# A two-layer decoder trunk: the first two gate/up units of stages 2 to 4 computed in token rows from split weights

## What is computed

```python
x = post_norm(x, 0.5 * swiglu(x, gate[0,0], up[0,0], down[0,0]), ...)   # stage 1
x = post_norm(x, pool_mixer(x), ...)
x = post_norm(x, 0.5 * swiglu(x, gate[0,1], up[0,1], down[0,1]), ...)   # stage 2
x = post_norm(x, 0.5 * swiglu(x, gate[1,0], up[1,0], down[1,0]), ...)   # stage 3
x = post_norm(x, swa_sink_attention(x), ...)
x = post_norm(x, 0.5 * swiglu(x, gate[1,1], up[1,1], down[1,1]), ...)   # stage 4
# swiglu(x) = (silu(x @ gate) * (x @ up)) @ down; gate, up 1024 x 2816, down 2816 x 1024
# post_norm(x, s) = layer_norm(sqrt(2) * x + s), per token over the 1024 channels
```

## Time and profile before

| | |
|---|---|
| median of three runs | 879.35 us |
| profiled execution, its own time | 879.61 us |
| its span, first to last instruction | 877.8 us |
| PE busy | 850.1 us (97%) |
| DVE busy | 561.1 us (64%) |
| ACT busy | 415.5 us (47%) |
| mean granted clock of TensorE | 0.995 |

### The profile page before, as it was taken

How to read it: one execution, slowest core, us unless ns; L and a number is a source line. 1 busy time by engine, 2 the same in 40 slices (tenths; PEclk the granted TensorE clock), 3 DMA queues, 4 the chain that set the end, 5 groups by cost and what they waited for, 6 DMA issues and landing times.

```text
span 877.8 us, 12580 instructions
## 1 busy us (share of the span) xinstructions
PE 850.1 (97%) x4712; PEld 727.4 (83%) x4712; DVE 561.1 (64%) x782; ACT 415.5 (47%) x654; POOL 25.6 (3%) x51
## 2 busy tenths in 40 slices
PE   7999999996999999999999999999989999999996
PEld 6888888886988888888888888887756988888885
DVE  2765565579655655657665655669787856656556
ACT  2555455432354554543454554554564544545540
POOL 0000000001100000001000000011000000000000
PEclk9999999999999999999999999999999999999998
DMA  9986547282585465563756556554145385565501
GB/s 280 351 295 224 184 155 230 72 266 97 193 295 181 160 226 177 168 223 109 238 197 203 180 191 194 189 192 144 49 139 197 104 301 174 189 200 182 191 1 49
DMA packets 116143, 162.19 MB, mean 185 GB/s; under 512 B 3936, under 2 KB 97632, under 8 KB 116112
## 3 DMA queue, kind: packets, MB, share of 16 engines
q1 hardware_dynamic: 112656, 152.06, 52.1%
q0 software_dynamic: 2496, 9.44, 3.1%
q10 hardware_dynamic: 960, 0.27, 0.1%
HBM read 160.70 MB, written 1.05 MB: 184 GB/s over the span
## 4 chain that ended last, share of the span: by engine, by line
PE 91%; DVE 6%; issue 1%; ACT 1%; DMA 1%; DVEq 0%; SPq 0%
PE ps L1083 28%; PE ps L1081 16%; PE ps L1034 10%; PE ps L1036 10%; PE ps L1035 10%; PE ps L1050 6%; PE ps L1080 4%; PE ps L1062 1%; PE ps L907 1%; PE ps L910 1%; PE ps L1115 1%; PE ps L916 1%; DVE xn L740 1%; DVE stats L746 1%; DMA raw_g<-in_ffn_w_gate 1%
## 5 line engine op out<-in xcount | busy, mean ns | idle before, releaser
L1083 PE MATMUL ps<-xT,g_hi 128*128 128x512 f32 x1064 | 379.3, 396 | 0.0
L1081 PE MATMUL ps<-xT,g_lo 128*128 128x256 f32 x1216 | 314.1, 279 | 0.0
L1081 PEld LDWEIGHTS ps<-xT,g_lo 128*128 128x128 f32 x1216 | 229.2, 188 | 12.8
L1083 PEld LDWEIGHTS ps<-xT,g_hi 128*128 128x128 f32 x1064 | 199.7, 188 | 41.2
L690 DVE TENSOR_TENSOR g_lo<-raw_g,g_hi 128x1024 fp32r<-128x1024 f32 x171 | 208.0, 1222 | 25.0 <-ACT g_hi L434 24.9
L700 DVE TENSOR_TENSOR gu<-ps,gu 128x512 f32<-128x512 f32 x76 | 52.6, 692 | 230.5 <-ACT gu L457 230.5
L434 ACT ACTIVATE g_hi<-raw_g 128x1024 fp32r<-128x1024 f32 x172 | 179.7, 1052 | 8.0 <-PE ps L916 3.7
L457 ACT ACTIVATE gu<-ps 128x512 f32<-128x512 f32 x76 | 45.6, 600 | 283.2 <-PE ps L1083 283.2
L1034 PE MATMUL ps<-d_hi,hT_hi 128*128 128x512 f32 x352 | 137.9, 392 | 0.6 <-DVE hT_lo L710 0.6
L1036 PE MATMUL ps<-d_hi,hT_lo 128*128 128x512 f32 x352 | 137.0, 389 | 0.0
L1035 PE MATMUL ps<-d_lo,hT_hi 128*128 128x512 f32 x352 | 137.0, 389 | 0.0
(11 more groups left out here) (128 smaller groups left out, 628.8 us busy)
## 6 DMA issues: line engine op xcount, KB each, us to landing
raw_d<-in_ffn_w_down SPq DMA_DIRECT2D x87, 512.0 KB, 4.0
raw_g<-in_ffn_w_gate SPq DMA_DIRECT2D x43, 1024.0 KB, 5.5
raw_g<-in_ffn_w_up SPq DMA_DIRECT2D x43, 1024.0 KB, 8.0
raw_g<-in_attn_w_qkv SPq DMA_DIRECT2D x6, 1024.0 KB, 6.2
raw_d<-in_attn_w_o SPq DMA_DIRECT2D x8, 512.0 KB, 3.7
gb<-in_ln_g POOLq DMA_DIRECT2D x6, 512.0 KB, 3.8
gb<-in_ln_b POOLq DMA_DIRECT2D x6, 512.0 KB, 5.5
xn<-in_x SPq DMA_DIRECT2D x2, 512.0 KB, 5.9
```

The lines of the kernel that those rows point to most:

```text
L1081: last = pe.matmul(bank[:, S:2 * S], w_lo, xT_hi[:, k, :], start=False, stop=False)
L1083: last = pe.matmul(bank, w_hi, xT[:, k, :, :], start=False, stop=k == KT - 1)
```

## The change

Units 0 and 1 of stages 2 to 4 no longer use raw weights. Their weights are split like the others, into two slots, one of them a new third slot of `g_hi` and `g_lo`; `gate_up_tokens` computes both units together for 128 tokens at a time, tokens on the partitions, 512 moving columns (2 units, gate and up, 128 channels each). ACT and DVE form h in token rows, PE transposes h (two transposes per t) into ACC[0][0], and ACT and DVE split it from there. PE then runs half of gate_up(2) before and half after the second pair of transposes. The copies into `xf` go in stages 2 to 4. Buffers are shared anew to make room (xf lies in qT, kd, rtmp, prevT and pT0 in kx, pT1 in gb, q_sb is halved), so the output bias is loaded into gb during attention, its `residual_bias` moves behind the chunks of q, and the layer-norm offset is loaded when the last values are done. `load_gate_up` of a stage is issued ahead of its first `load_down`.

Where the two new splits stand in the queues of ACT and DVE: for stage 2 after the pool mixer's `residual_bias` and ahead of its layer norm; for stage 3 and for q, k, v in unit 20 of the stage before, the second behind the `d_split` of unit 21 and ahead of unit 21's silu and h; for stage 4 in attention tasks 6 and 7. POOL's half split for q, k, v goes to ACT and DVE too.

```diff
-G_SLOTS = 2
+EXTRA = 2
+G_SLOTS = 3
+        def next_splits(f, u, it):
+            if 1 <= u < UNITS - 2:
+                return [(f, u + 2, it)]
+            if f in (1, 2) and u == UNITS - 2:
+                return [(f + 1 if f == 1 else None, v, 0) for v in range(2)]
+            return []
 # ACT, g_split: when the slot is free
-                    after(act, g_used, (G0[f] + u - 3 if f is not None and u < 4 else G - 1) + 4 * it)
+                    if f is None:
+                        after(act, g_used, G_QKV + (-1, 0, 0, 1, 3, 4)[u])
+                    elif f == 0:
+                        after(act, g_used, 0 if u < 4 else G - 1 + 4 * it)
+                    else:
+                        after(act, g_used, G0[f] + (-1, 0, 0, 2)[u] if u < 4 else G - 1 + 4 * it)
 # ACT and DVE, unit(): one split as before, the second at its end
                 if u + 1 < UNITS:
                     d_split(D0[f] + u + 1, it)
+                for a in ahead[1:2]:
+                    g_split(*a)
 # ACT, attention
+                if i >= len(TASKS) - 2:
+                    if i == len(TASKS) - 2:
+                        act.activation(sm[:, 0, 5, 0:1], mhalf[:, :], ACT.Silu)
+                    g_split(3, i - len(TASKS) + 2)
 # DVE, attention
-            chunk(1, 0)
-            chunk(1, 1)
+            dve.wait_ge(b_o_in, 16)
+            for t in range(TT):
+                chunk(1, t)
+                residual_bias(t, gb[:, 0, :])
...
+                if i >= len(TASKS) - 2:
+                    g_split(3, i - len(TASKS) + 2)
 # DVE, after the pool mixer
-                    layer_norm(1)
-                    for t in range(TT):
-                        x_lo(1, t)
-                    g_split(1, RAW_UNITS)
+                    g_split(1, 0)
+                    g_split(1, 1)
+                    enter(1)
+            def enter(f):
+                e = FFN_EVENT[f]
+                layer_norm(e, between=lambda: x_lo(e, 0))
+                x_lo(e, 1)
+                h_tokens(f, 0)
+                g_split(f, RAW_UNITS)
 # PE
+            def gate_up_tokens(f, t):
+                e, first = FFN_EVENT[f], g_slot(f, 0)
+                out_, tok = ps[:, WORK + 2 + t, :], slice(t * P, (t + 1) * P)
+                w_hi, w_lo = (b[:, first:EXTRA + 1:EXTRA - first, :].rearrange("p u (m k f) -> p u m k f", m=2, k=KT) for b in (g_hi, g_lo))
+                if t == 0:
+                    pe.wait_ge(g_lo_done, 2 * (X0[f] + 2))
+                for k in range(KT):
...
+                    pe.matmul(out_, xT_hi[:, k, tok], w_hi[:, :, :, k, :], start=k == 0, stop=False)
+                    pe.matmul(out_, xT_hi[:, k, tok], w_lo[:, :, :, k, :], start=False, stop=False)
+                for k in range(KT):
...
+                    last = pe.matmul(out_, xT_lo[:, k, tok], w_hi[:, :, :, k, :], start=False, stop=k == KT - 1)
-                    gate_up_raw(f, 0, 0)
-                    gate_up_raw(f, 1, 0, (0,))
+                    gate_up_tokens(f, 0)
                     transposes(e, 1)
-                    gate_up_raw(f, 1, 0, (1,))
-                    gate_up_raw(f, 0, 1)
-                    gate_up_raw(f, 1, 1)
-                ffn_down(f, 0)
+                    gate_up_tokens(f, 1)
+                    h_transposes(f, 0)
+                    gate_up(f, 2, ms=(0,))
+                    h_transposes(f, 1)
+                    gate_up(f, 2, ms=(1,))
+                    ffn_down(f, 0)
 # POOL
+                    gp.wait_ge(oT_ps, len(TASKS))
+                    load_offset(4)
```

More of the change, by code:

```diff
@@ L463, in unit @@
             def unit(f, u, it=0):
-                ahead = (f, u + 2, it) if 1 <= u < UNITS - 2 else (None, 0) if f == 2 and u == UNITS - 2 else None
+                ahead = next_splits(f, u, it)
                 if u not in DIRECT:
                     low_of(f, u, it)
-                if ahead and u not in DIRECT:
-                    g_split(*ahead, halves=(0,))
+                    for a in ahead[0:1]:
+                        g_split(*a, halves=(0,))
                     silu_of(f, u, it)
-                    g_split(*ahead, halves=(1,))
+                    for a in ahead[0:1]:
+                        g_split(*a, halves=(1,))
                 else:
                     silu_of(f, u, it)
-                    if ahead:
-                        g_split(*ahead)
+                    for a in ahead[0:1]:
+                        g_split(*a)
                 h_hi_of(f, u, it)
@@ L480, in unit, with silu_tokens, first_units, channel_major @@
                     d_split(D0[f] + u + 1, it)
-            def channel_major(e):
+                for a in ahead[1:2]:
+                    g_split(*a)
+            def silu_tokens(f, t):
+                act.wait_ge(*((tokens_done, f) if t == 0 else (g_used, G0[f] + 2)))
+                act.activation(gu[:, t, 0, :].rearrange("p (u f) -> p u f", u=2), tokens_bank(t)[:, :, 0, :], ACT.Silu).then_inc(silu_done, 1)
+            def first_units(f):
+                d_split(D0[f])
+                d_split(D0[f] + 1)
+                silu_tokens(f, 1)
+                g_split(f, 3, halves=(0,))
+                act.wait_ge(hT_ps, 2 * f)
+                slot = D0[f] % D_SLOTS
+                act.activation(hT_hi[:, slot:slot + 2, :], hT_bank(), ACT.Copy).then_inc(h_hi_done, 2)
+                g_split(f, 3, halves=(1,))
+                d_split(D0[f] + 2)
+            def channel_major(e, between=None):
                 for t in range(TT):
-                    for q, done in enumerate((xf_lo_done, xf_up_done)):
-                        if e != QKV_EVENT and (e > 0 or q == 1):
-                            act.wait_ge(tr_done, 4 * e + 2 * t + q + 1)
-                            act.activation(xf[:, t, 4 * q:4 * q + 4, :], x_bank(e, t, q).rearrange("p (k s) -> p k s", k=4), ACT.Copy).then_inc(done, 1)
+                    if e == 0:
+                        act.wait_ge(tr_done, 2 * t + 2)
+                        act.activation(xf[:, t, 4:8, :], x_bank(0, t, 1).rearrange("p (k s) -> p k s", k=4), ACT.Copy).then_inc(xf_up_done, 1)
                     for q in range(2):
@@ L504, in _ @@
             for f in range(FFNS):
-                d_split(D0[f])
-                for u in range(4):
+                if f == 0:
+                    d_split(D0[0])
+                else:
+                    first_units(f)
+                for u in range(2 if f > 0 else 0, 4):
                     unit(f, u)
@@ L915, in qkv @@
                         k = 4 * half + j
-                        last = pe.matmul(bank, xT_lo[:, k, tok], g_hi[:, X % G_SLOTS, 512 * j:512 * (j + 1)], start=False, stop=k == KT - 1)
+                        last = pe.matmul(bank, xT_lo[:, k, tok], g_hi[:, slot, 512 * j:512 * (j + 1)], start=False, stop=k == KT - 1)
                     return last
```

254 lines of the change are left out of this document (151 added, 103 removed).

## The result

The changed kernel takes 889.38 us (median of 4 runs, 889.06 to 890.3), the kernel before in the same comparison 879.65 (879.33 to 880.9): ratio 1.011, 95% interval 1.0092 to 1.0127. It is 9.7 us slower; I had forecast 4.6 to 4.9 slower, with 887.2 as the far end. The profiled execution has a span of 887.4 us, 9.6 more than before, and a mean granted clock of 0.987 against 0.995.

What follows compares the result with a forecast made beforehand. PE bounds the kernel (97% busy, 91% of the chain). Terms -7.2 + 4.5 + 4.6 - 1.2 + 3.6 + 0.6 = +4.9 on 879.61 us, 884.2 us as median; range 880.8 to 887.2.

Steps and rivals of the forecast that it cites:

- Token rows and start of attention, -8.4: Stages 2 to 4: token rows replace raw passes, -7.2 us; start of attention: PE's waits for low parts go, -1.2.
- The rival of closer matmuls: 512-column matmuls spaced closer than their columns take, 16 us less in three stages: 868 us; chance 0.01.
- Splits of stage 2, stage ends, task 7: Inserted splits delay PE: before stage 2's layer norm +4.5 us, ends of stages 2 and 3 +2.3 each, attention task 7 +3.6.
- the fast side's rivals: Inserted splits largely covered by ACT's and DVE's idle time, 875.5 us, chance 0.08; or part hidden, 880.2, chance 0.11.
- I take +0.6: Clock loss behind the tail's 4.2 us gap in task 7: +0.6 us, ends 0 and 1.3; stage 2's 1.3 kept.
- 0, other end 1.3 each: Clock loss behind the two 2.2 us gaps at the ends of stages 2 and 3: none, at most 1.3 us each.
- Cost 0, else up to 2: Last layer norm's offset load after values(7): in time at no cost; up to 2 us if it collides with a gate/up load.
- The rival "more clock loss": All gaps fall to 1.2 GHz, 4.6 us more, some 888.8 us at most, typically 887.5; chance 0.08.
- a sign that it would be wrong: Listed among the signs of being wrong: the last layer norm waits for its offset.

Runs made afterwards that it cites:

- the first experiment: Changed kernel, but ACT's high-part split for the second new unit (stage 3, q, k, v) waits only for unit 20's gate_up, not unit 21's: 885.33 us, ratio 1.0054.
- The repetition: The changed kernel run once more, unaltered: 890.03 us (888.72 to 893.54), ratio 1.0105.
- The filler: Changed kernel plus seven unused 512-column matmuls on constants in PE's 7.7 us gap before stage 2: 888.55 us, ratio 1.0094.
- the version with all three mends: Changed kernel with second splits behind unit 21's h, stage 2's low parts on POOL while DVE reads PSUM, stage 4's splits moved earlier: 871.36 us, ratio 0.9902.

## Why the prediction was wrong

Its mechanism was right, and the direction. Two terms of its sum were mis-sized, the two that I had put at or near nothing on the strength of one row each.

- **Token rows and start of attention, -8.4.** Right: -2.29 and -2.28 where nothing disturbed, -1.60 at the start of attention, and 8.7 us less than before when the inserted splits stood elsewhere. The rival of closer matmuls is out: stage 4's start took 13.88 us, and 13.84 were forecast from the rate of 24 matmuls in 5.58 us.
- **Splits of stage 2, stage ends, task 7: +4.5, +2.3 twice, +3.6.** Right to 0.1 us each: 4.54, 2.26 twice, 3.59, and each went away when its cause was moved. That the splits would be partly or wholly hidden, the fast side's rivals, did not happen, since the wait in ACT's queue was for the same matmul as silu's; with one unit less in that wait (the first experiment) it would largely have been.
- **The failed step: "I take +0.6" and, for the two gaps of 2.2, "0, other end 1.3 each".** The clock cost 4.4 us beyond that of before in the profiled execution: 1.2 in stage 2, 1.72 behind one of the two gaps of 2.1, 1.51 in task 7. The step went from two rows, that 3.2 us lost and 1.9 did not, to a bound between them. The repetition showed that there is none to be had from one execution: the gap of 1.94 us lost, and one of 2.10 lost where the other had before. Over all profiles the two long gaps, 7.7 and 4.2, lost every time, where the +0.6 had them at a part of the price, and of the two of 2.10 one lost every time. The filler showed that the loss is the gap's, 2.2 us gone with the same work. The rival "more clock loss" had the mechanism and the size (up to 4.6, here 3.8 more than the 0.6); it had deserved far more than 8 chances in 100, since all of its gaps were above the only one that I called free.
- **The second failed step: "Cost 0, else up to 2".** The offset load was late by 1.23 us. I had its issue, its 5.5 us and the collision, and took the edge case as no cost, when 5.5 against 6.1 left 0.6 to spare and the gate/up load came ahead of it. The load alone took 3.9 us, with company over 6, and it came behind the gate/up load partly because the values of task 7 ran at half clock. The prediction had named this wait as a sign that it would be wrong.
- Together 3.8 + 1.2, less 0.3 from the small differences, make the 4.7 us by which the span missed.

What stays open: why a gap of 2 us costs the clock in one execution and not in the next, and why of the two gaps of 2.10 always one fell. The Trainium skill ("TensorE: Matmul & The Clock Gate", "What's actually happening") says that the throttled state is the default one and that activity releases it; that half clock stood behind idle gaps fits, but no run here explains the choice among equal gaps.

## What to carry to other kernels

- When an engine's queue is in order, price a moved piece by the event that its wait is for: a split of 2 us in idle time is nearly free (the first experiment left 0.4 us of wait), and the same split with a wait for the event that its neighbour waits for costs all of it. Moving six of the new splits turned a loss of 9.7 us into a gain of 8.7.
- A new gap on TensorE has two prices, its length and the clock behind it. Here gaps of 3.2 us and more lost the clock every time and those of 1.9 to 2.1 in 16 of 43 cases, and a fall cost 1.5 to 1.7 us behind the gaps of 4.2 and less, or nothing where PE waited behind it anyway. Put that price in the sum, not at the edge of the range, and look at more than one execution before a gap is called free.
- Count a load's slack together with the load that may run beside it: here 0.6 us of slack was lost to a larger load issued 0.7 us ahead.

## What the hardware showed that I had not expected

POOL and DVE are not independent when both read two SBUF operands: two DVE instructions of 1.41 us took 5.61 us, as long as POOL's pair of 5.24, while the statistics, with one input, kept their 0.69 beside POOL. And executions of one program on one core can differ by 5 us, mostly in company with the mean granted clock: 883.1 us at 0.991 and 888.2 at 0.986, or 889.6 at 0.987 and 893.5 at 0.982. It is no fixed rate: the version with all three mends took 871.15 us at 0.996 and 871.18 at 0.992.
